# The last two feed-forward blocks in one accumulation, modulation columns in three places, and attention values in banks that no score waits for

## The reference

```python
mods = jnp.split(c_act @ w_ada[i] + b_ada[i], 6, axis=-1)
u = x * (1.0 + sc1) + sh1
y = mixer(u)                                   # gla_mixer, then chunk_attention
x = layer_norm(ALPHA * x + (1.0 + g1) * y, ...)
u = x * (1.0 + sc2) + sh2
y = jnp.square(jax.nn.relu(u @ ff_w1[i])) @ ff_w2[i]     # 1024 -> 4096 -> 1024
x = layer_norm(ALPHA * x + (1.0 + g2) * y, ...)
```

## Time and profile before

| | us |
|---|---|
| median of 3 runs | 1918.57 (1912.75 to 1918.66) |
| profiled execution, its time | 1917.75 |
| its span, first to last instruction | 1916.0 |
| TensorE busy | 1822.1 (95%) |
| VectorE busy | 1201.7 (63%) |
| GpSimd busy | 802.0 (42%) |
| ScalarE busy | 756.5 (39%) |
| mean granted clock of TensorE | 0.975 |

### The profile page before, as it was taken

How to read it: one execution, slowest core, us unless ns; L and a number is a source line. 1 busy time by engine, 2 the same in 40 slices (tenths; PEclk the granted TensorE clock), 3 DMA queues, 4 the chain that set the end, 5 groups by cost and what they waited for, 6 DMA issues and landing times. The chain is left out here.

```text
span 1916.0 us, 25156 instructions
## 1 busy us (share of the span) xinstructions
PE 1822.1 (95%) x9203; PEld 1468.8 (77%) x9203; DVE 1201.7 (63%) x1783; ACT 756.5 (39%) x1189; POOL 802.0 (42%) x577
## 2 busy tenths in 40 slices
PE   4999999999999999998999999999999999999999
PEld 3877687788888777777788888877788777777877
DVE  5777557876777851654597777778388733216552
ACT  2343444322322333554432222325334555545551
POOL 4433235565565343321356565652423333342212
PEclk8999999899999999999899999998999999999999
DMA  8534425555554233221355555441211222321211
GB/s 335 198 119 133 144 89 187 170 178 170 172 170 138 87 110 99 67 89 55 121 194 171 172 165 166 163 142 46 98 56 50 69 66 88 111 82 63 66 56 66
DMA packets 123049, 235.72 MB, mean 123 GB/s; under 512 B 8112, under 2 KB 37680, under 8 KB 121936
## 3 DMA queue, kind: packets, MB, share of 16 engines
q1 hardware_dynamic: 119920, 227.17, 36.3%
q10 hardware_dynamic: 3040, 7.34, 1.1%
HBM read 232.36 MB, written 2.13 MB: 122 GB/s over the span
## 5 line engine op out<-in xcount | busy, mean ns | idle before, releaser
L2232 POOL TENSOR_TENSOR wsp<-raw,wsp 128x512 fp32r<-128x512 f32 x528 | 791.1, 1530 | 1094.1 <-ACT wsp L189 1094.1
L226 PE MATMUL bank<-xT,wsp 128*128 128x512 f32 x2592 | 611.1, 396 | 10.5 <-POOL wsp L2232 5.6
L226 PEld LDWEIGHTS bank<-xT,wsp 128*128 128x128 f32 x2592 | 490.7, 190 | 123.6 <-issue 8.8
L189 ACT ACTIVATE wsp<-raw 128x2048 fp32r<-128x2048 f32 x132 | 252.0, 1913 | 557.2 <-PE bank L452 248.1
L452 PE MATMUL bank<-wsp,hT 128*128 128x512 f32 x1344 | 320.4, 399 | 5.6 <-POOL wsp L2232 3.4
L226 PE MATMUL bank<-wsp,xT 128*128 128x512 f32 x1248 | 305.6, 400 | 8.9 <-ACT hf L2282 4.5
L452 PEld LDWEIGHTS bank<-wsp,hT 128*128 128x128 f32 x1344 | 255.1, 190 | 68.7 <-issue 5.4
L226 PEld LDWEIGHTS bank<-wsp,xT 128*128 128x128 f32 x1248 | 234.1, 191 | 65.3 <-issue 6.9
L553 DVE TENSOR_TENSOR h<-h 128x512 f32<-128x512 f32 x64 | 57.3, 910 | 79.9 <-ACT h L510 79.6
L570 DVE TENSOR_TENSOR htmp<-bank,gate 128x512 f32<-128x512 f32 x112 | 76.8, 686 | 47.4 <-PE bank L452 47.4
L1314 PE MATMUL bank<-xT,wsp 128*128 128x512 f32 x384 | 103.0, 413 | 0.0
(11 more groups left out here) (306 smaller groups left out, 2115.6 us busy)
## 6 DMA issues: line engine op xcount, KB each, us to landing
raw<-in_ff_w SPq DMA_DIRECT2D x64, 1024.0 KB, 5.6
ada_ring<-in_w_ada SPq DMA_DIRECT2D x48, 384.0 KB, 3.7
ada_ring<-in_ada_w SPq DMA_DIRECT2D x48, 384.0 KB, 3.9
ring<-in_w_ada SPq DMA_DIRECT2D x64, 256.0 KB, 3.4
raw<-in_odd_w_in SPq DMA_DIRECT2D x16, 1024.0 KB, 5.5
raw<-in_gla_w_in SPq DMA_DIRECT2D x12, 1024.0 KB, 5.6
raw<-in_att_w_in SPq DMA_DIRECT2D x12, 1024.0 KB, 5.2
raw<-in_even_w_in SPq DMA_DIRECT2D x12, 1024.0 KB, 5.2
```

What stands on the lines that cost most here:

```text
L189: act.activation(wsp[:, slot, 0], raw[:, slot], ACT.Copy).then_inc(hi_made, 1)
L226: mm = pe.matmul(out_ap, l, r, start=(start and n == 0), stop=(stop and n == 2))
L2232: ins = pool.tensor_tensor(wsp[:, slot, 1, k], raw[:, slot, k], wsp[:, slot, 0, k].bitcast(F32), ALU.subtract)
```

## The change

- **Pair.** Hidden blocks 6 and 7 are multiplied in one accumulation: for n = 0, first block 6 (slot 0), then block 7 (slot 1), both into banks 4 to 7; for n = 1, per tile block 6 then block 7, into banks 0 to 3. VectorE evicts and adds once per tile and n (`add_pair`). SyncE loads the four W2 halves in that order.
- **Columns 0 to 15** of both layers come in the pair, behind the first half of tile 0 of n = 1. The rows come behind the pair, in layer 1 columns 24 to 39 behind the rows.
- **Columns 24 to 39 of layer 0's `modacc`** come in attention units 27 and 28, eight each, in bank 6; their fold ahead of `att_out`'s results.
- **Value panels** of both attentions go to banks in the order `V_BANK`; scores 0 wait for none (`att_in`) or two of the value evictions, scores 1 for all, and ScalarE evicts value tile 3 ahead of the conversion.
- **`even_in`.** The second panel takes the plain order, its tile 3 is evicted ahead of the conversion, the first HGRN pieces wait for their own bank alone. Ahead of it, one conversion goes behind `act_root` of tile 3, the other behind block 3 of the turning.

```diff
+            def down_pair():
+
+                i, j = FB - 2, b + 4 * FB - 4
+                for q, h in enumerate((hT[l], xT)):
+                    pe.wait_ge(s["hT_ready"], 4 * (i + q) + 4)
+                    for t in range(ST):
+                        if q == 0:
+                            pe.wait_ge(s["acc_done"], 16 * i - 8 + 2 * t + 1)
+                        mm = down_tile(h, j + q, q, t, ST + t, q == 0, q == 1)
...
+                pe.wait_ge(s["relu_done"], 4 * FB)
                 for t in range(ST):
+                    for q, h in enumerate((hT[l], xT)):
+                        mm = down_tile(h, j + 2 + q, q, t, t, q == 0, q == 1)
...
+                        if t == 0 and q == 0:
+                            pe.wait_ge(s["ada_used"], KT * FB)
+                            pe.wait_ge(s["acc_done"], 16 * i + 1)
+                            pe_modcols(pe, modacc[l], range(16), ST, mod_done)
...
-            with pe.Fori(1, FB - 1) as i:
+            with pe.Fori(1, FB - 2) as i:
                 up(i + 1)
                 down(i)
...
-            down_last()
-            r1, r2 = mod_rows[l]
+            up(FB - 1)
+            down_pair()
+            pe.wait_ge(mod_made, (5, 8)[l])
+            for r, off in enumerate(mod_rows[l]):
+                pe.wait_ge(s["acc_done"], 16 * (FB - 2) + 2 * r + 2)
+                pe_modrow(pe, modacc[l], off, ST + 2 * r, mod_done)
+            pe.wait_ge(s["acc_done"], 16 * (FB - 2) + 2 * ST)
             if l:
-                pe_modcols(pe, acc, [*range(16), *range(24, 40)], HK - 1, mod_done, at=SEQ - P)
...
+                pe_modcols(pe, modacc[l], range(24, 40), HK - 1, mod_done, at=SEQ - P)
...
-            step(FB - 2, last=True)
-            before_last()
-            dve.wait_ge(s["acc_done"], 16 * (FB - 1))
+            ada(FB - 1, range(0, 4))
+            square(FB - 1)
+            low(FB - 1, xT)
+            ada(FB - 1, range(4, 8))
             for t in range(ST):
-                add_last(t)
+                add_pair(0, t)
+            before_pair()
+            for t in range(ST):
+                add_pair(1, t)
                 if affine:
                     affine(t)
```

`pe_panels`, `act_evac`, `pe_transposes_by_tile`, `act_transposed`, attention and HGRN:

```diff
-                                 b == 0 and isinstance(i, int), b == 1 and len(runs) == 1)
+                                 b == 0 and isinstance(i, int), b == 1 and kind == "NN")
...
-                    if t == 3:
-                        act_ahead(act, name, 2 * i + b, 1)
+                    if t == 3 and b == 0:
+                        act_ahead(act, name, 2 * i, 1)
...
+            act_ahead(act, name, 2 * i + 1, 1)
...
-                if k == HK and between:
+                if k == min(ahead, HK) and between:
                     between()
...
+                if k == HK and at_half:
+                    at_half()
...
+        V_BANK = (2, 3, 0, 1)
...
-                pe.wait_ge(free, free_at + t + 1)
+                pe.wait_ge(free, free_at + order[t] + 1)
...
+                if u == 1:
+                    pe.wait_ge(TS[ts]["bank_free"], KT + ST * PHASE0[name])
...
-            pe.wait_ge(TS[ts]["bank_free"], KT + ST * PHASE0[name])
+            v_made = KT + ST * (PHASE0[name] - 1)
+            if name == "odd_in":
+                pe.wait_ge(TS[ts]["bank_free"], v_made + 2)
...
+                if u in columns:
+                    pe.wait_ge(TS[ts]["bank_free"], KT + ST * PHASE0[name] + 4 * ST)
+                    pe_modcols(pe, modacc[0], columns[u], D_BANK, mod_done if columns[u][-1] == 39 else None)
...
-                    if t == 3:
+                    if t == 3 and seq < 2:
                         act_ahead(act, "att_in", seq, 1)
...
+            act_ahead(act, "att_in", 2, 1)
...
-                        pe.wait_ge(free, KT + 2 * ST)
+                        pe.wait_ge(free, KT + ST + HD_BANK - ST + t + 1)
...
-            act_root(act, "ff1", 0)
-            for t in range(1, ST):
+            for t in range(ST):
                 act_root(act, "ff1", t)
-                act_rms(act, "even_in", t - 1)
-            act_rms(act, "even_in", ST - 1)
-            for slot in range(2):
-                act_high(act, base["even_in"] // 2, slot)
-
-            act_transposed(act, "in_even_in", scale_at, bias_at)
+                if t == ST - 1:
+                    act_high(act, base["even_in"] // 2, 0)
+                act_rms(act, "even_in", t)
+
+            act_transposed(act, "in_even_in", scale_at, bias_at, lambda: act_high(act, base["even_in"] // 2, 1))
...
-            pe_transposes_by_tile(pe, "hid_ff1", 1, KT - 1, lambda: pe.wait_ge(mod_made, 7),
-                                  lambda: pe_modcols(pe, modacc[0], range(24, 40), LAST_COLUMNS, mod_done, at=SEQ - P))
+            pe_transposes_by_tile(pe, "hid_ff1", 1, KT - 1)
             pe_ff(pe, 1)
-            pe_transposes_by_tile(pe, "in_even_in", 1, HK - 1, lambda: pe.wait_ge(mod_made, 9), lambda: pe.wait_ge(mod_made, 8))
+            pe_transposes_by_tile(pe, "in_even_in", 1, HK - 1, lambda: pe.wait_ge(mod_made, 9))
```

More of the change, by code:

```diff
@@ L609, in step @@
                 add(i, 1, peel)
-                if not last:
-                    low(i + 1, hT[l])
+                low(i + 1, hT[l])
             ada(0, range(KT))
@@ L1358, in pe_out @@
                 pe_out_piece(pe, s, name, 0, t, h)
+            if name == "att_out":
+                pe.wait_ge(mod_made, 7)
             for t, h in LAST_FIRST:
```

137 lines of the change are left out of this document (67 added, 70 removed).

## The result

| | before | after |
|---|---|---|
| time, median (lowest to highest) | 1913.48 us (1912.01 to 1918.66) | 1900.56 us (1899.27 to 1904.49), 5 runs |
| ratio | | 0.9928 [0.9914, 0.9942] |
| profiled execution, span | 1917.75, 1916.0 us | 1899.27, 1897.5 us |
| mean granted clock | 0.975 | 0.979 |

The changed kernel is 0.7% faster. The forecast was 1896.0 us (1888.5 to 1906.0); the median is 4.6 us above it. The sum was made on profiled executions: 23.1 us off 1917.75. The profile after shows 18.5 us off, spans compared. Between medians 22.6 us were forecast and 12.9 measured. The rest of that distance is the median of before, which was 1918.57 in the three runs ahead of the prediction and 1913.48 here; in the next timing of the same two kernels (`e0`) it was 1916.27 and the difference 17.7 us.

What follows compares the result with a forecast made beforehand. TensorE, busy 95% of the span, was taken as the bound. Gains of 1.5 + 3.2 + 4.0 + 4.2 + 3.2 + 7.0 = 23.1 us off 1917.75, plus 0.8 to the median, gave 1896 us (1888.5 to 1906).

Steps and rivals of the forecast that it cites:

- one of its own signs of being wrong: Attention units 0 to 2: a wait for `aP` or `fP` of over 1 us would show the forecast wrong.
- the slow stretches at 747, 1379 and 1717: Half-clock stretches at the first attention, HGRN start and second attention, forecast to be gone.
- the one at 638: Slow-clock stretch behind layer 0's feed-forward columns, forecast to be there still.
- 1: Feed-forward pair, layer 0: `htmp` wait goes and clock loss shrinks; gain 1.5 us (0.7 to 2.4).
- 2: Feed-forward layer 1 and start of `even_in`: +1.9 until the last matmul, then 15.3 for 20.4; -3.2 us (-5.9 to +0.6).
- 3: First attention's value panel: wait for the value eviction and slow clock behind it go; gain 4.0 us (2.5 to 4.3).
- 4: Second (forgetting) attention's value panel: the same wait of 2.6 us and clock go; gain 4.2 us (2.5 to 4.3).
- Free: First attention, unit 0: softmax behind the conversion starts at +2.8 us, probabilities due about +5.5, so no cost.
- rival A: Both attentions' first units give the gain back through ScalarE's order: 1.7 instead of 8.2 us, 1902 us; chance 0.12.
- 5: `att_out` to `hid_ff1`, columns into units 27 and 28: 5.4 us saved, part paid back; net 3.2 us (1.8 to 5).
- 6: Start of HGRN: first piece's 4.5 us wait and 2.9 us of slow clock go; gain 7.0 us (4.5 to 7.4).
- The slow clock by chance: Whole kernel: all slow stretches shift against the clock, 2 us to either side.

Runs made afterwards that it cites:

- e0: The changed kernel timed again, unchanged: 1898.61 us, ratio 0.9917 to the kernel before.
- e5: Changed kernel with fifteen of the sixteen columns in the feed-forward pair left out in both layers: 1894.01 us, ratio 0.9880 to the kernel before.
- e1: Changed kernel with columns 24 to 39 moved from the attention units back behind `att_out`: 1900.19 us, ratio 0.9918 to the kernel before.
- e2: Changed kernel with ScalarE converting the unit weights behind unit 0's softmax in both attentions: 1900.89 us, ratio 0.9918 to the kernel before.
- f3: Changed kernel with modulation tiles requested first, squares ahead of residual, columns 24 to 39 in the key panel, conversion behind unit 2's softmax: 1902.63 us, 0.9929.
- e7: Changed kernel with each feed-forward stage's first three modulation tiles requested ahead of the second block's upward weights: 1891.78 us, ratio 0.9875 to the kernel before.
- e3: Changed kernel with the `even_in` and HGRN-start part undone: 1906.52 us, ratio 0.9956 to the kernel before.
- f0: Changed kernel with VectorE's squares and low parts of block 0 ahead of the residual in both feed-forward stages: 1909.33 us, ratio 0.9969 to the kernel before.

## Why the prediction was right, and where it was not

The forecast held because each wait that it named did go and TensorE's line shortened at each of the places but one; the sizes were off in both directions, and one of its own signs of being wrong came true (under 3). Of what it named as signs, the slow stretches at 747, 1379 and 1717 are gone in the profile after, the one at 638 too, which was to stay. By its steps, each measured between one profile of before and one or two after:

- **1** (-1.5, measured -4.4, or -2.8 in executions with a slow stretch). The wait for `htmp` went, nothing took its place. Mis-sized: the 2.5 us of clock for the columns, which cost 0 to 1.6 there; `e5` has the columns themselves at 1.07 us net at full clock. The -4.4 is 1.1 us of wait and 3.3 of clock, and clock is partly luck: eight of twelve profiles with this pair have a slow stretch in it, the changed kernel's two don't. (By its own terms the step's range is 0.5 to 2.3, not 0.7 to 2.4.)
- **2** (-3.2, measured -7.4). Until the last matmul I had +1.9, the pair gave -1.1 (clock again); the tail gave -6.3 for -5.1. VectorE's chain is as worked out: the statistics end 2.6 us behind the last matmul, for 2.8, and the panel comes 14.1 us behind it, for 15.3.
- **3** (-4.0, measured -2.1). Up to the scores 79.28 (`e0`, `e1`) against 81.78 before, and +0.4 behind them (192.62 in `e1` against 192.25); the changed kernel's own profile has -0.7, with a longer slow stretch in the panel.
- **4** (-4.2, measured -2.9: -2.6, and 199.88 in `e0` against 200.15). What failed in 3 and 4 is "Free": I counted ScalarE's order and not who stands beside VectorE. GpSimd's low parts had ended when VectorE normalised; with the eviction wait gone they overlap, and 0.48 became 2.13 us. The 1.10 us wait for `aP` in unit 1 is over the 1 us that I had named as a sign of being wrong. Together that is half of rival A, by another cause than A names (`e2`, `f3`). The softmax of the second attention was at 1702.98 behind its table load from 1701.69 for 1.28 us, so the row held there: nothing of 1.38 us stands behind the load, nor ahead of it, where the conversion ends at 1701.67.
- **5** (-3.2, measured +1.9 up to the first hidden tile, 6.2 - 4.3, and +5.2 behind). Two terms failed. "Two groups, 1.8 us paid, plus 0.4 for clock" was 6.2 us: of the 3.6 us of columns 1.8 lay in the wait, which leaves 1.8, and 10.2 us more at half clock, at 1.6 us for 3.4, are 4.8, together 6.6 and 0.4 too many. In the kernels whose clock was at half for less it was 4.5. And the 4.3 us won behind `att_out` were no gain: `ff1`'s first downward product hung on SyncE's queue and VectorE, not on TensorE, and took it back (`e7`). I had asked what is late next at the join, and not at the first product behind it, 30 us on.
- **6** (-7.0, measured -8.2, and 7.7 by `e3`). The new 1.01 us wait is inside.
- **The slow clock by chance** (2 us to either side): the profile after has 1.5 us of luck in the second attention, and none of the slow stretches that other kernels have in pair 0, in pair 1 and behind the level matmuls (172.7 for 171.1 us), 1.6 us each.

Errors of both signs met: 2.9, 4.2 and 1.2 us more gain in 1, 2 and 6; 3.3 and 1.3 less in 3 and 4 and 10.3 less in 5. With the 1.5 us of luck and 0.5 ahead of the pair that is 18.5 for 23.1: the sum came out better than its terms, and that is luck. Between medians it was further off: 22.6 us forecast, 12.9 and 17.7 measured.

The Trainium skill ("SBUF — State Buffer", SBUF: two separate sides) has GpSimd and VectorE share one port pair as an exclusive lock, held for a whole instruction; on VectorE's side it names operations in a two-port mode and those with two inputs in SBUF. The trace agrees in kind: each of the two steps takes about 1.1 us for 0.24, while one of GpSimd's four instructions takes 1.25. Which mode these steps run in no run here shows. Had I weighed it in parts 3 and 4, the sum would have been about 3 us smaller (0.88 + 1.10 - 0.28 and 0.48 + 0.96 - 0.28, the 0.28 being waited before too).

## What to carry to other kernels

A wait that is removed moves every engine's work against its neighbours': look not only for what is late next, but at which engines now run side by side, and follow the gain to the next place where TensorE meets a transfer queue. Ask for small, early-needed tiles ahead of large ones in an in-order queue; that one reordering brought more than half as much as the whole change. When a chain of one engine is long, putting one consumer first can make another late (`f0`); starting the chain earlier helped (`e7`).

## What the runs showed of the hardware

- Sixteen one-column matmuls took 3.2 to 3.6 us in the attention units, at a granted clock of 0.50 (1.2 GHz) for all but the first 0.4 us, where twice as many took 3.63 us at full clock in the feed-forward pair.
- Slow stretches of 3.4 us come and go at the same instructions, 1.6 us each: between two executions of one program (6.8 and 3.4 us behind the key panel's weight wait), and between kernels whose instructions there are the same (pair 1: 47.63, 49.2 or 50.8 us).
- Single-source VectorE steps of 128x128 were 4.4 times as long beside GpSimd's tensor operations (2.13 against 0.48 us for two), and residual operations of 128x1024, with two inputs, 1.8 times (2.2 against 1.23). In `e2` a cast of 128x512 took 1.51 us beside them, for 0.42 without.
